# A rising FFN projection by Strassen's seven block products, with the falling projection after it

## What is computed

```python
x = x + memory_attend(...)                     # ends in o @ w_mem_o, 512 -> 1024
h = rmsnorm(x) * g_ffn                         # 1024 features
u = h @ w_up                                   # 1024 -> 5632
c = b_conv + u[t-2]*w0 + u[t-1]*w1 + u[t]*w2   # causal, per feature
a, b = split(c, 2)                             # 2816 features each
x = x + (silu(a) * b) @ w_down                 # 2816 -> 1024
y = rmsnorm(x) * g_final
```

## Time and profile before

| | |
|---|---|
| time, median of 3 runs | 1693.03 us (1692.85 to 1693.12) |
| span of the profiled execution, first to last instruction | 1691.4 us |
| instructions | 26509 |
| DMA | 119.41 MB, mean 71 GB/s |
| granted TensorE clock, mean | 0.998 of full speed |

### The profile page before, as it was taken

How to read it: one execution, slowest core, us unless ns; L and a number is a source line. 1 busy time by engine, 2 the same in 40 slices (tenths; PEclk the granted TensorE clock), 3 DMA queues, 4 the chain that set the end, 5 groups by cost and what they waited for, 6 DMA issues and landing times.

```text
span 1691.4 us, 26509 instructions
## 1 busy us (share of the span) xinstructions
PE 1667.8 (99%) x10487; PEld 1544.0 (91%) x10487; DVE 1060.9 (63%) x1438; ACT 529.6 (31%) x960; POOL 500.1 (30%) x231
## 2 busy tenths in 40 slices
PE   9999999999999999999999999999999999999998
PEld 8999889676667799998999999999999999999997
DVE  7583587896667654536676655565655656565566
ACT  7320222686566531214333121111202021120222
POOL 2683132000000124430333433334333333343332
PEclk9999999999999999999999999999999999999999
DMA  5322220330313223316211111111111111111113
GB/s 208 103 75 82 82 63 14 115 94 1 113 51 99 83 95 122 111 36 272 88 46 41 38 50 37 49 38 37 50 37 43 44 37 50 37 39 47 38 48 112
DMA packets 36334, 119.41 MB, mean 71 GB/s; under 512 B 6049, under 2 KB 9345, under 8 KB 33953
## 3 DMA queue, kind: packets, MB, share of 16 engines
q1 hardware_dynamic: 33952, 108.89, 19.9%
q10 hardware_dynamic: 2304, 9.44, 1.6%
HBM read 100.86 MB, written 15.17 MB: 69 GB/s over the span
## 4 chain that ended last, share of the span: by engine, by line
PE 93%; DVE 3%; ACT 1%; issue 1%; POOL 1%; DMA 0%; SPq 0%; DVEq 0%; ACTq 0%; POOLq 0%
PE scores L2118 35%; PE bank L2118 35%; PE scores L2424 3%; PE bank L2484 3%; PE scores L2214 2%; PE bank L2508 2%; PE bank L2127 1%; PE scores L2136 1%; DVE kbuf L1755 1%; PE bank L2779 1%; PE scores L2447 1%; PE bank L2542 1%; PE bank L2538 1%; PE scores L2757 1%; PE bank L2501 1%
## 5 line engine op out<-in xcount | busy, mean ns | idle before, releaser
L918 POOL TENSOR_TENSOR w_hi<-w_raw,zero 128x1024 fp32r<-128x1024 f32 x96 | 188.0, 1959 | 1098.2 <-PE bank L2118 464.0
L2118 PE MATMUL scores<-act_hi,w_hi 128*128 128x384 f32 x920 | 310.2, 337 | 0.9 <-POOL w_lo L921 0.9
L2118 PE MATMUL scores<-act_lo,w_hi 128*128 128x384 f32 x920 | 309.1, 336 | 0.0
L2118 PE MATMUL scores<-act_hi,w_lo 128*128 128x384 f32 x920 | 309.1, 336 | 0.0
L921 POOL TENSOR_TENSOR w_lo<-w_raw,w_hi 128x1024 fp32r<-128x1024 f32 x96 | 253.5, 2640 | 7.6
L2046 DVE TENSOR_TENSOR x<-bank,x 128x384 f32<-128x384 f32 x216 | 120.5, 558 | 103.6 <-PE bank L2118 103.6
L2118 PE MATMUL bank<-act_hi,w_hi 128*128 128x384 f32 x544 | 183.8, 338 | 0.9 <-POOL w_lo L921 0.9
L2118 PE MATMUL bank<-act_hi,w_lo 128*128 128x384 f32 x544 | 182.8, 336 | 0.0
L2118 PE MATMUL bank<-act_lo,w_hi 128*128 128x384 f32 x544 | 182.8, 336 | 0.0
L2118 PEld LDWEIGHTS scores<-act_hi,w_hi 128*128 128x128 f32 x920 | 173.0, 188 | 2.5 <-POOL w_lo L921 1.5
L2118 PEld LDWEIGHTS scores<-act_lo,w_hi 128*128 128x128 f32 x920 | 173.0, 188 | 0.0
(11 more groups left out here) (402 smaller groups left out, 3095.0 us busy)
## 6 DMA issues: line engine op xcount, KB each, us to landing
w_raw<-wstream SPq DMA_DIRECT2D x106, 512.0 KB, 3.6
x_blk<-xT ACTq DMA_DIRECT2D x8, 576.0 KB, 4.6
x_mid<-x_blk ACTq DMA_DIRECT2D x8, 576.0 KB, 3.1
x<-x_mid SPq DMA_DIRECT2D x4, 1152.0 KB, 5.5
z<-cache_k SPq DMA_DIRECT2D x4, 1024.0 KB, 5.3
z<-cache_v SPq DMA_DIRECT2D x4, 1024.0 KB, 7.3
mk_c<-mk_c SPq DMA_DIRECT2D x4, 1024.0 KB, 11.6
mv_c<-mv_c SPq DMA_DIRECT2D x4, 1024.0 KB, 14.2
```

What stands on the lines that cost most here:

```text
L918: pool.tensor_tensor(w_hi[:, k], w_raw[:, k], zero[:].unsqueeze(2).to_broadcast([P, KB, P]), ALU.add).then_inc(w_rounded, 1)
L2118: mm = pe.matmul(out, w[:, k, at + kb], x(kb), start=first and kb == 0 and n == 0, stop=last and kb == n_kb - 1 and n == 2)
```

## The change

**Work of a unit.** A unit is one hidden block u with both halves, a and b. The 1152 frames are four quarters of QF = 288; the pairs of quarters (0, 1) and (2, 3) are p = 0 and 1. For each p the product of a 2 x 2 block matrix of weights (a or b by K rows 0 to 3 or 4 to 7) with a 2 x 2 block matrix of activations (K rows by quarter) is made by seven block products i = 0 to 6 instead of eight. Each has 4 K blocks in three fp32r matmuls of 288 columns: 12 matmuls. Products 0, 2, 4, 5 go on adding in bank p; ACT copies the bank out after 0, 2 and 4 (`hold`), and after 5 into `ext` (`hold_first_columns`); DVE adds a held copy to banks 2 + p and 4 + p (`join`).

**Operands.** The seven weight operands need four sums or differences of raw blocks of 128 x 512 (`up_sum_1` to `up_sum_4`) and seven splits (`round_up` on ACT, `up_low` on DVE; on POOL for units 0 and 1). POOL does nothing in the loop over the units. The seven activation operands for each p are made once: x is scaled by the reciprocal root and the gain first (`scale_rows`), then four sums (`combine`), and seven splits of 128 x 1152 elements (`round_part`, `split_part`).

**Order.** The memory output goes by quarters: 32 tiles of 288, first both quarters of p = 0, then those of p = 1; slots of two weights are loaded and split a second time. Sums of squares, roots and scaling are made once for each half. Units 0 and 21 do all of p = 0 before p = 1 ("turned"); units 1 to 20 take p inside i, in a loop of 10 rounds.

**Through DRAM.** The x rows are stored to `x_mid` by SP (`store_x`), since x is overwritten, and read again as `xd` for the falling projection. The gated rows go to `s_mid` (`store_s`) and come back per group (`load_s`); ACT rounds and DVE subtracts them there (`round_hidden`, `split_hidden`). All of the falling projection follows the last unit; it has the tiles, matmuls and widths of before, with eight banks in turn, and POOL splits its weights.

```diff
+MO_ROWS = ((0, 1), (2, 3), (6, 7), (4, 5))
+MO_LAST = {3: 0, 7: 1, 19: 2, 23: 3, 27: 4, 31: 5}
+MO_SUMS = 18
+SCALE_AFTER = {19: (0, 1), 20: (2, 3), 21: (4, 5), 22: (6, 7)}
+SPLIT_IN_MO = {23: 0, 25: 1, 27: 2, 29: 3, 30: 4}
+SUM_IN_MO = {24: (0, 1), 26: (2,), 28: (3,)}
...
 # PE
+            def half_sums(p):
+                pe.wait_ge(x_summed, 2 * KB + 7 * p + 7)
...
+            def up_product(u, i, p, turned=False):
+                pe.wait_ge(up_ready, 7 * u + i + 1)
+                if first:
+                    pe.wait_ge(x_split, 2 * KB + 7 * p + i + 1)
+                acc = (0, 2, 0, 4, 0, 0, 4)[i] + p
...
+                if i in (2, 4, 5):
+                    pe.wait_ge(held, held_no(u, (2, 4, 5).index(i), p, turned))
+                for kb in range(4):
+                    for n, (w, b) in enumerate(((0, hi), (0, lo), (1, hi))):
+                        mm = pe.matmul(bank[acc][:, 0:QF], up_w[i][:, w, tile(kb)], b[:, kb], ...)
+            for p in range(2):
+                for i in range(7):
+                    up_product(0, i, p, True)
+                    if p == 0 and i == 1:
+                        half_sums(1)
+            with pe.Fori(0, NFF // 2 - 1) as i:
+                unit(2 * i + 1)
+                unit(2 * i + 2)
...
 # ACT, one unit of the loop
+                first_tap(u - 1, 0)
+                round_up(u, par, g, 6)
+                hold(u, 0, 0); hold(u, 0, 1)
+                round_up(u + 1, 1 - par, next_g, 0)
+                activate(u - 1)
+                round_up(u + 1, 1 - par, next_g, 1)
+                hold(u, 1, 0); hold(u, 1, 1)
+                round_up(u + 1, 1 - par, next_g, 2)
+                round_up(u + 1, 1 - par, next_g, 3)
+                hold(u, 2, 0); hold(u, 2, 1)
+                round_up(u + 1, 1 - par, next_g, 4)
+                hold_first_columns(u, 0); hold_first_columns(u, 1)
+                round_up(u + 1, 1 - par, next_g, 5)
+                first_tap(u, 1)
 # DVE, one unit of the loop
+                up_low(u, par, 6)
+                more_taps(u - 1, 0)
+                fill_carried(u, 0)
+                join(u, 0, 0)
+                up_low(u + 1, more, 0)
+                gate(u - 1)
+                join(u, 0, 1)
+                up_sum_3(u + 1, more, next_g)
+                up_sum_2(u + 1, more)
+                up_low(u + 1, more, 1)
+                up_low(u + 1, more, 2)
+                up_sum_1(u + 1, more)
+                up_low(u + 1, more, 3)
+                fill_carried(u, 1)
+                join(u, 1, 0); join(u, 1, 1)
+                up_low(u + 1, more, 4)
+                up_low(u + 1, more, 5)
+                up_sum_4(u + 1, more)
+                join(u, 2, 0); join(u, 2, 1)
+                more_taps(u, 1)
 # DVE between the memory output and unit 1
+            for d in range(MO_EARLY + 1, N_MO):
+                memory_residual(d)      # add_square after 11, 13, 15, 16; half_inverse(0) after 19
+                ...                     # then scale_rows, split_part, combine by the tables above
+            split_part(0, 5)
+            split_part(0, 6)
+            join(0, 0, 0, True)
+            half_inverse(1)
+            scale_rows(1, (0, 1, 2, 3))
+            scale_rows(1, (4, 5, 6, 7))
+            join(0, 1, 0, True)
+            split_part(1, 0)
+            split_part(1, 1)
+            combine(1, 0)
+            combine(1, 1)
+            join(0, 2, 0, True)
+            split_part(1, 2)
+            combine(1, 2)
+            join(0, 0, 1, True)
+            combine(1, 3)
+            for i in range(3, 7):
+                split_part(1, i)
 # POOL between the memory output and unit 1
+            up_sum_3(0); up_sum_2(0); up_low(0, 0..2); up_sum_1(0); up_sum_4(0)
+            split_again(W_MO + 4)
+            add_square(1); add_square(2)
+            split_again(W_MO + 5)
+            add_square(3..7)
+            up_low(0, 3..6)
+            up_sum_3(1); up_sum_2(1); up_low(1, 0..2); up_sum_1(1); up_low(1, 3..5); up_sum_4(1)
 # SP
+            load_s(0)                   # after product (21, 6) of p = 0
+            for n in range(4):
+                sp.dma_start(xd[:, 2 * n:2 * n + 2], io["x_mid"][:, 2 * n:2 * n + 2])
+            store_s(NFF - 2)
+            load_s(1)
+            store_s(NFF - 1)
```

More of the change, by code:

```diff
@@ L898, in _ @@
+            store_s(NFF - 1)
+            sp.wait_ge(product, product_no(NFF - 1, 6, 1, True))
+            sp.wait_ge(conv_moved, 16 + 32 * NFF)
+            load_s(NGRP - 1)
+            for g in range(NGRP - 1):
+                for k in range(2):
+                    load_down(2 * g + 2 + k)
+                if g + 2 < NGRP - 1:
+                    sp.wait_ge(w_used, W_END + 2 * g + 2)
+                    load_s(g + 2)
             sp.wait_ge(tap0_done, 2 * NFF)
@@ new lines, in join @@
+            def join(u, j, p, turned=False):
+                ab, h, acc, of, after = ((0, 0, 2 + p, kept_a, 0), (1, 1, 4 + p, kept_a, 2), (0, 1, 4 + p, kept_b, 1))[j]
+                dve.wait_ge(product, product_no(u, (1, 3, 6)[j], p, turned))
+                dve.wait_ge(held, held_no(u, after, p, turned))
+                for dst, (a, b) in up_pieces(ab, 2 * p + h, (bank[acc], of[:, p])):
+                    last = dve.tensor_tensor(dst, a, b, ALU.add)
+                last.then_inc(joined, 1)
```

824 lines of the change are left out of this document (601 added, 223 removed).

## The result

The changed kernel took 1698.02 us (median of 7, 1695.49 to 1699.77), the kernel before 1693.03 us on the same chip: ratio 1.0027, 95% interval 1.0017 to 1.0037. That is slower, a little beyond what can be told from no change; 1680 and faster was forecast. The unedited kernel was measured twice more, as the control of later series: 1693.61 us, ratio 1.0003 (0.9994 to 1.0012), and 1694.98 us, ratio 1.0007 (0.9998 to 1.0016). So its median depends by some 4 us on the occasion, where the medians of the kernel before lie between 1693.0 and 1693.4 us, and its gain over the kernel before is nothing or slightly negative. What has to be explained is the 13 to 18 us by which the forecast was too low.

What follows compares the result with a forecast made beforehand. PE's matmuls set the time, other engines hidden. Terms -56.3 + 1.3 + 25.3 + 3 + 6 + 5 + 3 = -12.7 on the 1691.4 us span gave 1678.7, or 1680.3 as median; own range 1667 to 1692, with rivals 1659 to 1704.

Steps and rivals of the forecast that it cites:

- the start of the falling projection: After the last unit: late second activation load and DVE's split make PE wait; +3 us, bounds 1 and 6.
- the stall from memory output to unit 1: PE waits on DVE's work, lengthened by POOL: 27 us, less 1.7 before, so +25.3; bounds 15 and 36.
- the clock: PE may fall to half clock behind two long stalls between memory output and unit 1: +3 us, bounds 0 and 19.
- the last unit: Unit 21, all p = 0 before p = 1: uncovered holds and a SiLU before the second; +5 us, bounds 2 and 7.
- Matmuls: Rising projection: more but narrower matmuls at 133.3 ns, 549.1 to 492.8 us, -56.3; memory output +1.3.
- Rival 5: A matmul of 288 columns costs 3 ns more than the line says: 11 us more, 1691; chance 0.03.
- The ring: Units 1 to 20: engines waiting for each other in a cycle, 21.95 us against PE's 22.4; +6 us, bounds 0 and 25.
- Rival 2: Units 1 to 20: the engines' cycle of waits becomes the bound, costing 28 us in place of 6: 1702; chance 0.17.
- The second sum: PE's sum of the second half's squares in unit 0, expected 51.5 us after the seventh memory output tile without POOL's interference.
- Rival 3: The clock stays down behind both long stalls before unit 1: 17 us in place of 3, 1694; chance 0.10.
- Rival 1: Everything is covered: stall 20, POOL and DVE rarely collide, no clock loss; -32.7 us, 1660; chance 0.15.
- Rival 4: Memory output to unit 1: POOL blocks DVE for all its 30 us, stall 49 in place of 27, 1702; chance 0.07.

Runs made afterwards that it cites:

- e6_narrow: Changed kernel with POOL's two weight splits and seven sums of squares cut to 8 columns: unit 0 ended 6.4 us earlier, median 8.2 us lower.
- e8_fill: Changed kernel plus dummy matmuls in three PE waits of unit 0: second sum of squares to unit 0's last join 36.6 us instead of 37.3.
- e12_last: Changed kernel with ACT's second held copy ahead of the SiLU in the last unit: 2.4 us less in units 1 to 21 and in the median.
- e4_sp: Changed kernel with SP storing unit 20's rows before the residual loads and loading falling weights 2 and 3 earlier: 8.1 us under the unedited changed kernel.
- e13_act: Changed kernel with two first-half squares on ACT ahead of three weight roundings: eleven runs from 1689.65 to 1693.98 us.
- e3_sums20: Changed kernel with PE's first-half sum of squares behind memory output tile 20 instead of 18: 1.6 us under the unedited changed kernel.

## Why the prediction was wrong

The forecast was a gain, and there was none. The saving was sized rightly; what failed are three terms of cost: most of all the start of the falling projection (3 forecast, 10.4 measured), where SP's order was not followed to its end; then the stall from memory output to unit 1 (27 and 3 for the clock, against 39.8 in the first profile and 33.8 in the control); and, by little, the last unit (5, against 6.5). The steps, with the changed kernel's own profile:

- *Matmuls, -56.3, and 133.3 ns for 288 columns: right.* In memory output 95 starts lie between these two rows: 12.61 us / 95 = 132.7 ns. Rival 5 is out.

```profile
815.48 0.30 PE L2647 MATMUL scores<-om_hi,w_hi 128*128 128x288 f32 x1
...
828.09 0.29 PE L2647 MATMUL scores<-om_hi,w_lo 128*128 128x288 f32 x1
```

- *The ring of units 1 to 20, +6: the number right, in part by luck.* 453.9 us against 448.0 of matmuls, +5.9. The forecast spread 0.3 us over every unit. In the trace units 2 to 20 take 22.39 and 22.73 us in turn, so the ring costs nothing in one and 0.3 in the other, 2.9 in all, and the other 3.0 are in unit 1, where PE waits 1.2 and 1.3 us for ACT's held copies; that unit was not priced by itself. No row stood behind the 0.05 us assumed for most hand-overs; the trace gives no sign that it was too small. The taps take what was assumed, where in the earlier trace rows the median of the first was 3014 ns beside POOL. Rival 2 is out.

```profile
L2466 DVE SCALAR_TENSOR_TENSOR conv<-ext,consts,conv x44: 1423/1434/2302, 918.5 to 1409.6; 128x1168 f32<-128x1168 f32 x44
```

- *From memory output to unit 1, 27 and 3 for the clock: too low.* From the seventh tile to the end of unit 0 104.4 us against 64.6 without pauses: 39.8 in the first profile, over the bounds of 15 and 36, and 33.8 in the control, inside them. The second sum was due at 51.5 us behind that tile without POOL; e6_narrow gives 54.6, the control 61.6. So POOL's 7 us were the middle of the guess, and 3 were missing in DVE's and PE's row. From the second sum to the second half 13.5 us were forecast and 18.1 measured, in the first profile and in the control. The missing step is the one at 891.70 above: product 6 of the first half waits for a join that DVE's order puts behind the reciprocal and all eight scalings, which I had counted as beside it. A scaling also took 0.81 us at the median where 0.75 was assumed, and the eight together 7.92, 1.4 more than that, with POOL beside them. From there to the end 19.5 were forecast, 19.9 measured in the first profile and 19.0 in the control.
- *The clock, +3:* it fell (0.78 from 877 to 915 us) and e8_fill shows that it cost under 1 us in that part. Rival 3, 17 us behind those two stalls, is out. The clock did cost time where the forecast did not look, behind two other waits: 1.35 us in unit 21 in this profile and none in the control's, 2.6 us at the start of the falling projection. In the first profile, where the wait before the first sum was 3.0 us instead of 0.8, the part from that sum to product 0 took 33.7 us instead of 31.4 with the lower clock; that part was not tested.
- *Last unit, +5:* 28.9 us against 22.4, +6.5, with the SiLU before the second hold, as said; 27.5 us in the control, +5.1, the difference being the clock. e12_last took 2.4 us of it away.
- *Start of the falling projection, +3 with bounds of 1 and 6: the step that failed most.* The stretch of e4_sp, where only SP's order differs, is 10.4 us shorter than the changed kernel's and 11.1 shorter than the control's. That is what this order costs, and all that the start costs: e4_sp has no pause left there. The prediction priced when the activations arrive and took the rest of SP's queue as free. It missed that the next weights stand behind `store_s(NFF - 1)`, so behind the last gate, and that four loads issued within 2.1 us land after 12.4 us at the median, not after the 5.5 of the earlier trace rows, where the four are issued over 33 us, with unit 20's store behind them landing after 15.9 and 18.5 us.

With the measured terms the forecast's sum becomes -56.3 + 1.3 + 38.1 (39.8 - 1.7) + 5.9 + 6.5 + 10.4 = +5.9; the span grew by 6.1. Rival 1 never had a chance with DVE's row as long as this. Rival 4 (POOL takes all its 30 us) had its time right, 1702 against 1698, for the wrong reason: POOL cost 7 us. What stays open is the spread between occasions. The profiles show pieces of it: a late transfer, which by e13_act does not carry it alone, and a clock that falls behind a wait in some executions and not in others, worth 1.35 us in unit 21 and 1.4 in the falling stretch (1.5 us behind the second wait in e3_sums20, 2.9 in the control). The 4 us between the medians were not taken apart further.

## What to carry to other kernels

At a hand-over between two phases write down every engine's order as one list, SP's too, and ask of each instruction what stands ahead of it that waits for something later. A wait that an engine shows is worth only what the bound behind it allows: two waits shortened by 2.4 and 2.7 us ahead of DVE's row brought nothing measurable, work taken off DVE came back about one for one, and a wait of the last unit, with no such row behind it, came back whole. Where the tensor engine waits anyway, let it do the sums that two vector engines would fight over.

## What the runs showed of the hardware

A DVE instruction with two SBUF operands that meets one of POOL's waits for what is left of it. In the control two scalings took 3.99 us beside POOL's instructions of 1.95 and 2.41, and 1.54 alone. A residual add, which reads one operand from PSUM, kept its 0.45 us (849.39) beside POOL's 848.93. It goes the other way round too: a DVE add of 1.11 us kept its length and POOL's instruction beside it took 1.80 us instead of 1.28. The rows of DVE and of POOL in the control:

```profile
826.99 1.11 DVE L2359 TENSOR_TENSOR stat<-stat 128x576 f32<-128x576 f32 x1
...
843.66 1.54 DVE L2369 SCALAR_TENSOR_TENSOR x<-x,consts,stat 128x576 f32<-128x576 f32 x2
...
845.48 3.99 DVE L2369 SCALAR_TENSOR_TENSOR x<-x,consts,stat 128x576 f32<-128x576 f32 x2
849.39 0.45 DVE L2352 TENSOR_TENSOR x<-scores,x 128x288 f32<-128x288 f32 x1
```

```profile
821.94 1.28 POOL L1181 TENSOR_TENSOR up_sum<-up_raw 128x512 f32<-128x512 f32 x1
...
827.45 1.80 POOL L1185 TENSOR_TENSOR up_raw<-up_raw,up_sum 128x512 f32<-128x512 f32 x1
...
844.54 1.95 POOL L1193 TENSOR_TENSOR stat<-stat 128x576 f32<-128x576 f32 x1 [3.60 <-ACT stat L1680]
846.45 2.41 POOL L1115 TENSOR_TENSOR w_hi<-w_raw,zero 128x1024 fp32r<-128x1024 f32 x1
848.93 2.75 POOL L1118 TENSOR_TENSOR w_lo<-w_raw,w_hi 128x1024 fp32r<-128x1024 f32 x1
```

The Trainium skill (SBUF — State Buffer, Who interferes with whom) says that whichever of the two starts first has the shared ports for its whole instruction; by that rule, the trace agrees in both directions. Not all of such work counts in the total: POOL was busy for 39 us of the 66 from the seventh tile to the second sum in the changed kernel's profile, and cutting down 24 of them, the two splits and the seven sums, won 7.
